# First block of a two-block network on one core: constants in two parts, additions ahead of the last split, table load behind the rounding of x

## What is computed

```
for l in range(2):
    h = rmsnorm(x, attn_norm[l])
    proj = h @ w_in[l]                       # 2048 columns in the kernel's layout
    y_a = mla_attention(...)                 # 4 heads, causal, with rope
    y_b = short_gated_conv(...)
    y_c = multiscale_pool(...)
    y_d = swa_sink_attention(...)            # window 128, with sinks
    mixed = group_norm([y_a, y_b, y_c, y_d]) * mix_norm[l]
    x = x + mixed @ w_o[l]
    gate, up = split(rmsnorm(x, ffn_norm[l]) @ w_gate_up[l])
    x = x + (silu(gate) * up) @ w_down[l]
x = rmsnorm(x, final_norm)
```

## Time and profile before

| | |
|---|---|
| median of 3 runs | 2251.24 us (2248.23 to 2251.54) |
| the profiled execution | 2254.26 us, span 2252.9 us |
| TensorE busy, products | 1946.3 us, 86% of the span |
| TensorE busy, weight loads | 1380.0 us, 61% |
| VectorE busy | 829.0 us, 37% |
| ScalarE busy | 650.2 us, 29% |
| GpSimd busy | 53.2 us, 2% |
| mean granted clock of TensorE | 0.917 of full |

### The profile page before, as it was taken

How to read it: one execution, slowest core, us unless ns; L and a number is a source line. 1 busy time by engine, 2 the same in 40 slices (tenths; PEclk the granted TensorE clock), 3 DMA queues, 4 the chain that set the end, 5 groups by cost and what they waited for, 6 DMA issues and landing times. The chain is left out here.

```text
span 2252.9 us, 41452 instructions
## 1 busy us (share of the span) xinstructions
PE 1946.3 (86%) x17860; PEld 1380.0 (61%) x17868; DVE 829.0 (37%) x1585; ACT 650.2 (29%) x1138; POOL 53.2 (2%) x58
## 2 busy tenths in 40 slices
PE   5989989899959755799999999597557899999995
PEld 5889988799959634644444444296347444444443
DVE  4766666666656533511111111264434211111112
ACT  3554444544444331211111111233312111111111
POOL 0400002200000000000000000000000000000000
PEclk9999999999989865799999999798658899999998
DMA  6245552345424002579999999340015699999992
GB/s 248 94 142 188 184 195 94 131 154 186 166 80 149 1 3 76 227 309 428 428 428 428 428 429 429 126 151 1 2 60 230 275 429 429 428 428 428 428 428 114
DMA packets 48565, 539.69 MB, mean 240 GB/s; under 512 B 6161, under 2 KB 7217, under 8 KB 7985
## 3 DMA queue, kind: packets, MB, share of 16 engines
q1 hardware_dynamic: 48432, 537.80, 58.8%
HBM read 536.73 MB, written 1.05 MB: 239 GB/s over the span
## 5 line engine op out<-in xcount | busy, mean ns | idle before, releaser
L2427 PE MATMUL experts_psG<-weights_gu,experts_xc 128*64 128x512 f32 x2048 | 450.8, 592 | 0.0
L2427 PEld LDWEIGHTS experts_psG<-weights_gu,experts_xc 128*64 128x64 f32 x2048 | 147.9, 137 | 292.1 <-issue 291.8
L2361 DVE TENSOR_TENSOR experts_sig<-experts_sig,experts_psG 128x256 f32<-128x256 f32 x64 | 27.0, 421 | 804.2 <-ACT experts_sig L2382 804.2
L404 DVE TENSOR_TENSOR ring_low<-ring_raw,ring_high 128x1024 fp32r<-128x1024 f32 x180 | 224.7, 1250 | 177.0 <-ACT ring_high L398 155.8
L2450 PE MATMUL experts_psD<-weights_d,experts_hT 128*64 128x512 f32 x1024 | 233.8, 598 | 1.6 <-ACT experts_hT L2390 1.6
L398 ACT ACTIVATE ring_high<-ring_raw 128x1024 fp32r<-128x1024 f32 x180 | 189.2, 1054 | 158.2 <-PE ffn_ps L515 91.3
L513 PE MATMUL ffn_ps<-first_x_high,ring_high 128*128 128x256 f32 x704 | 198.2, 282 | 0.0
L515 PE MATMUL ffn_ps<-first_x_high,ring_low 128*128 128x256 f32 x704 | 197.7, 281 | 0.0
L514 PE MATMUL ffn_ps<-first_x_low,ring_high 128*128 128x256 f32 x704 | 197.0, 280 | 0.0
L2450 PEld LDWEIGHTS experts_psD<-weights_d,experts_hT 128*64 128x64 f32 x1024 | 68.2, 136 | 131.9 <-issue 131.9
L2382 ACT ACTIVATE experts_sig<-experts_psG 128x256 f32<-128x256 f32 x64 | 24.6, 384 | 402.6 <-PE experts_psG L2427 402.6
(11 more groups left out here) (470 smaller groups left out, 3309.9 us busy)
## 6 DMA issues: line engine op xcount, KB each, us to landing
weights_gu<-in_moe_gate SPq DMA_DIRECT2D x64, 2048.0 KB, 14.0
weights_gu<-in_moe_up SPq DMA_DIRECT2D x64, 2048.0 KB, 18.5
weights_d<-in_moe_down SPq DMA_DIRECT2D x64, 2048.0 KB, 16.7
ring_raw<-in_w SPq DMA_DIRECT2D x90, 1024.0 KB, 4.8
project_w_raw<-in_w_in SPq DMA_DIRECT2D x22, 1024.0 KB, 5.0
output_w_raw<-in_w_out SPq DMA_DIRECT2D x8, 1024.0 KB, 8.6
const<-in_const SPq DMA_DIRECT2D x1, 2496.0 KB, 18.2
project_w_raw<-in_w_in SPq DMA_DIRECT2D x2, 1056.0 KB, 5.1
```

The lines of the kernel that those rows point to most:

```text
L404: dve.tensor_tensor(self.low[:, n % AHEAD], self.raw_half(n), self.high[:, n % AHEAD], ALU.subtract)\
L2427: ins = pe.matmul(out, xc[:, kk], wgu[:, par, kk, :, j * S:(j + 1) * S], start=kk == 0, stop=kk == DT - 1)
```

## The change

`load_while_split` gets a limit, so that the opening stage issues the first weight unit, then the first 256 columns of the constants with a semaphore of their own, then the other three units, then the rest of the constants. `PreNorm.sum` waits for the first part alone. In mix0 VectorE no longer waits for the constants at its start but ahead of the rope products, behind the split of half 7; it splits x first and then halves 0 to 3. ScalarE rounds x first, loads the tables, and then rounds halves 0 to 3; in mix1 as well the table load stands behind the rounding of x. In mix and in ffn the last split of the stage moves behind the four additions.

```diff
--- before.py
+++ after.py
@@ -375,9 +375,10 @@
         self.used = self.sem("used")
         self.issued = 0
 
-    def load_while_split(self, sp, splits):
-
-        while 2 * self.issued < N_ALL1 and (self.issued < self.SLOTS or 2 * (self.issued - self.SLOTS + 1) <= splits):
+    def load_while_split(self, sp, splits, most=N_ALL1):
+
+        while 2 * self.issued < N_ALL1 and self.issued < most and \
+                (self.issued < self.SLOTS or 2 * (self.issued - self.SLOTS + 1) <= splits):
             g = self.issued
             if g >= self.SLOTS:
                 sp.wait_ge(self.split, 2 * (g - self.SLOTS + 1))
@@ -424,6 +425,7 @@
         self.rstd = self.sb("rstd", [P, S])
         self.x_loaded = self.sem("x_loaded")
         self.vec_loaded = self.sem("vec_loaded")
+        self.ones_loaded = self.sem("ones_loaded")
         self.const_loaded = self.sem("const_loaded")
 
 
@@ -437,8 +439,11 @@
             def _(sp):
                 sp.dma_start(f.vecs[:], a["vec1"].rearrange("l p n -> p l n")).then_inc(f.vec_loaded, 16)
                 sp.dma_start(k.x[:], a["x_t"].rearrange("p (t s) -> p t s", t=DT)).then_inc(f.x_loaded, 16)
+                ring.load_while_split(sp, 0, 1)
+                early = 2 * P
+                sp.dma_start(k.const[:, 0:early], a["const"][:, 0:early]).then_inc(f.ones_loaded, 16)
                 ring.load_while_split(sp, 0)
-                sp.dma_start(k.const[:], a["const"]).then_inc(f.const_loaded, 16)
+                sp.dma_start(k.const[:, early:], a["const"][:, early:]).then_inc(f.const_loaded, 16)
 
             @block.vector
             def _(dve):
@@ -490,7 +495,7 @@
 
     def sum(self, pe):
         if self.first:
-            pe.wait_ge(self.f.const_loaded, 16)
+            pe.wait_ge(self.f.ones_loaded, 16)
         for t in range(DT):
             pe.wait_ge(self.squares, t + 1)
             ins = pe.matmul(self.bank[:, 0:S], self.k.c("ones"), self.f.sq[:, t], start=t == 0, stop=t == DT - 1)
@@ -681,12 +686,9 @@
                         dve.wait_ge(g_rounded, 2 * i + j + 1)
                         dve.tensor_tensor(low[:, j], y[:, t], high[:, j], ALU.subtract).then_inc(g_split, 1)
 
-                if first:
-                    dve.wait_ge(f.const_loaded, 16)
-                    ring.rest(dve, 0)
                 norm.rest(dve)
                 if first:
-                    for n in range(1, AHEAD):
+                    for n in range(AHEAD):
                         ring.rest(dve, n)
                 ring.rest(dve, base + 4)
                 evacuate(0)
@@ -697,6 +699,8 @@
                 dve.tensor_tensor(sq[:, 0:3], proj[:, T_CQ:T_CQ + 3], proj[:, T_CQ:T_CQ + 3], ALU.mult)\
                     .then_inc(latent_sq, 1)
                 ring.rest(dve, base + 7)
+                if first:
+                    dve.wait_ge(f.const_loaded, 16)
                 cos, sin = k.c("rope")[64:96, :], k.c("rope")[96:128, :]
                 ch.link(dve.tensor_tensor(rot[64:96, 0], proj[96:128, T_KR], sin, ALU.mult))
                 ch.link(dve.tensor_tensor(rot[64:96, 1], proj[64:96, T_KR], cos, ALU.mult))
@@ -750,7 +754,7 @@
                 ring.rest(dve, base + 21)
                 group(2)
                 group(3)
-                for n in range(22, 28):
+                for n in range(22, 27):
                     ring.rest(dve, base + n)
                 for b in range(4):
                     if b < 3:
@@ -759,6 +763,7 @@
                         dve.wait_ge(ring.used, base + N_MIX1)
                     xb = k.x[:, 2 * b:2 * b + 2].rearrange("p a s -> p (a s)")
                     dve.tensor_tensor(xb, xb, ps[:, b], ALU.add).then_inc(added, 1)
+                ring.rest(dve, base + 27)
 
             @block.scalar
             def _(act):
@@ -806,12 +811,10 @@
                         act.wait_ge(g_normed, 2 * i + j + 1)
                         act.activation(high[:, j], y[:, 2 * G_ORDER1[i] + j], ACT.Copy).then_inc(g_rounded, 1)
 
+                norm.round(act)
                 act.preload_act_table_set("natural_log_exp_and_others")
                 if first:
-                    ring.round(act, 0)
-                norm.round(act)
-                if first:
-                    for n in range(1, AHEAD):
+                    for n in range(AHEAD):
                         ring.round(act, n)
                 norm.square(act)
                 norm.scale(act)
@@ -1057,7 +1060,8 @@
                             dve.wait_ge(norm.rstd_ready, 1)
                         dve.tensor_tensor(gu[:, i % 2], bank(i).rearrange("p (a s) -> p a s", a=2), bc(f.rstd[:], 2, 1),
                                           ALU.mult).then_inc(scaled, 1)
-                    ring.rest(dve, base + n + AHEAD)
+                    if n < len(order) - 1:
+                        ring.rest(dve, base + n + AHEAD)
                     if what == "up":
                         dve.wait_ge(sig_ready, i + 1)
                         dve.wait_ge(scaled, i + 1)
@@ -1072,6 +1076,7 @@
                         dve.wait_ge(ring.used, base + len(order))
                     xb = k.x[:, 2 * b:2 * b + 2].rearrange("p a s -> p (a s)")
                     dve.tensor_tensor(xb, xb, ps[:, b], ALU.add).then_inc(added, 1)
+                ring.rest(dve, base + len(order) - 1 + AHEAD)
 
             @block.scalar
             def _(act):
```

## The result

The changed kernel takes 2233.95 us (median of 5 runs, 2232.68 to 2239.28) where the one before takes 2251.24 (5 runs, 2248.16 to 2253.06): a ratio of 0.9938, 95% interval 0.9919 to 0.9957. Faster, by 0.4 to 0.8%. The profiled execution took 2237.45 us with a span of 2236.1.

A forecast was written before the change was run, and what follows sets the result against it. The opening was taken as bound by VectorE's wait for the constants, stage changes by additions after the last split, mix1's start by a table load. 10.0 + 3.45 + 1.28 = 14.7 us off 2251.24 gave 2236.5, range 2230.5 to 2241.5.

The forecast's parts named there:

- What bounded the opening: Opening: VectorE's wait for constants it doesn't read holds everything some 10 us; removing it gains 10.0 us, between 8.6 and 10.9.
- The extra table load: Opening: ScalarE's first Copy gets a 1.28 us load from 6.15 to 7.43, ending 0.4 us behind x's landing.
- The rival that it isn't hidden: Opening: the extra load runs behind x's landing, 0.9 us later than assumed; 2237.4 us, chance 0.12.
- The squares and the later halves: Mix0's opening: three more halves on ScalarE to 16.3, squares done at 18.9, before TensorE starts the sums at 19.5.
- The moved wait: Rope products, about 34: constants land at about 23, 11 us to spare; slower rival if landing after 34, chance 0.02.
- The additions: Three stage changes: additions before the last split start the next stage 1.15 us earlier each, 3.45 us, at most 4.8.
- The load in mix1: Mix1's start: table load behind the rounding of x starts TensorE 1.28 us earlier; up to 2.4 with early clock.
- The sum: Whole kernel: 10.0 + 3.45 + 1.28 = 14.7 us, carried to the end.
- first three cases: Forecast (0.62), clock stays up (0.18) and extra load not hidden (0.12), all faster by more than 0.2%.
- the fourth: Opening: another limit the wait covered; half of part 1 gone gives 2241.5 us, all of it 2246.5; chance 0.06.
- The clock rival: Stage changes: TensorE's clock stays up, gaining 0.85 us per ffn stage, up to 1.1 in mix1; 2233.7 us, chance 0.18.
- The rule on table loads: Opening and mix1: a switch costs 2.66 us with drain, giving 2237.8; the prediction went by the rows' 1.28 instead.

The follow-up runs named there:

- the second: The changed kernel, nothing altered, profiled and measured once more: 2240.91 us against 2253.40 for the kernel before, ratio 0.9947.
- the opening alone: Changed kernel with the additions and mix1's table load put back as before, so only the opening's part remains: 2241.45 us against 2249.74, ratio 0.9968.
- warmed: Combined kernel plus products of zeros on TensorE where it waits (13 in the opening, 14 after mix0, ffn0 and mix1): 2229.84 us, ratio 0.9906; again 2231.22, 0.9905.
- combined: Changed kernel with mix0's table load first, half 0 amid x, mix1's load behind the squares, each stage's last weight unit issued in the next: 2232.94 us, ratio 0.9917.
- half 0 first: Changed kernel with, in mix0, the table load first, then half 0, then x on ScalarE and VectorE: 2235.38 us, ratio 0.9927.

## Why the prediction was right, point by point

- **What bounded the opening.** Right: the wait for the constants alone. Lead at mix0's Ln 10.13 us in the profile of the changed kernel, 10.56 in the second and 9.90 for the opening alone, against 10.0. The wait was worth more than that: with the order of the kernel before kept, 12.0 us at the Ln. The prediction took the new order as given and never asked what it costs; it cost 1.9, most of it the second table load.
- **The extra table load.** It exists (line 473), it stands ahead of the wait for x, and ends some 0.1 us behind x's landing. The rival that it isn't hidden is out. The stage was entered at 6.37 and not at 6.15, so the rounding of x began at 7.67 and not at 7.43, and the first product stands at 14.65 instead of 14.35. The preload's 1.28 us held in the sum, which adds lengths without their overlap.
- **The squares and the later halves** held nobody, as forecast: the squares are done at 18.64, the sums run from 19.34.
- **The moved wait.** No idle time at 34.33. Its price had it come too late was mis-sized, one for one against the 0.55 measured; it did not enter the sum.
- **The additions.** 1.15 us each was forecast, with SyncE's issue as the new last thing; 1.15, 1.13 and 1.15 were measured, and moving that issue gave 0.48 us more, against 0.45.
- **The load in mix1.** 1.28 forecast; 1.29 at the first product, 0.87 at the Ln, where a different rise of the clock stands in between.
- **The sum.** 14.7 forecast, 14.4 and 15.1 at the loop. In the first profile the parts are 10.13 us (opening), 3.43 (three stage starts) and 1.38 (mix1), less 0.50 that the two ffn stages lost, 0.25 each from their start to their Ln. The prediction had no term for this loss; in the ffn stages it looked at the clock only as something to gain. That the small misses cancel is luck. Two details of its working don't add up: its own bounds give 13.3 to 17.0 us, not 13.1 to 16.9, and with chances of 0.92 for the first three cases, 0.94 leaves only a third of the fourth, not most of it. Neither changes the forecast or the range.
- **The last step, from the sum to the time.** The median fell by 17.3 us in the first measurement and by 12.5 in the second. The forecast lies between, and neither gap to it is explained by the change: the second block alone took 1602.9 us in the trace of before and 1600.6 and 1604.0 in the two of the changed kernel. That the forecast of 2236.5 was missed by 2.6 us is within what these runs spread (2232.7 to 2239.3); a hit so close is partly luck.
- **The clock rival.** Its condition did not come: with TensorE's idle at 3.92 us (4.3 forecast) the clock still fell. Its price for an ffn stage, 0.85, fits the trace that it was read from: to their Ln the two took 8.79 and 8.86 us before and 7.99 and 8.00 warmed. But the stretch at half speed can start and end later, which the price left out: against the changed kernel the warmed one gains 1.05 and 1.11 us, against the combined one up to 1.95. For mix1 up to 1.1 was allowed, and 1.66 was measured against the changed kernel.
- **The rule on table loads.** The Trainium skill (ScalarE: Activation LUTs, What ACT_TABLE_LOAD costs) gives 2.66 us for a switch with its drain. Moving the load off the path in the opening gained 1.40 us, and putting one back in mix1, where Sigmoid's tables had been in place, moved the first product by 1.29, so here the traces do not agree. The times can't decide it: the forecasts with and without the drain, 2237.8 and 2236.5, lie closer together than the runs.

## What to carry to other kernels

Look at what a wait stands in front of, not at what it is for: one wait on 2.5 MB of constants, of which 128 KB were needed, held a whole core for 12 us, though the profile put the idle on another name. When such a wait goes, check anew in which order the engine ahead should work; here the new order put all of x and a second table load ahead of the weights, and lost 1.9 of the 12 us, most of it to the load. And when the last instruction of a stage is moved, follow its queue-mates: a 0.33 us issue of a transfer, covered before, became the end of the stage.

## What the runs showed of the hardware

- A table load that isn't in the code was put ahead of the first Copy of the program, 1.28 us; the explicit one behind it cost 1.40 between two instructions. With the explicit load first (half 0 first, 6.08) there was only that one.
- TensorE's clock cost more than the trace of before let me think. After idle times of 3.92 us (changed kernel), 3.82 us (combined kernel, at the change to ffn0) and more it was at half for up to 5.6 us of an ffn stage, though in the changed kernel TensorE had resumed at full clock and the fall came 0.7 us later; with products of zeros in the gap, and 0.40 us of idle, it stayed full. Three stages' starts then took 8.0 us each, in both traces, where the same work had taken between 8.8 and 10.1 (mix1 with a table load ahead of it left out).
- The second block, with the same code and data, took 1594.7 to 1610.3 us in thirteen traces. What moves it was not examined and stays open.
